# Opening of a diffusion block kernel: constants, modulation and first norm put into one stage

## The chip, the cores and the metric

The kernel runs on one core of a Trainium2 chip. The metric is the device time of one execution in microseconds (us), lower is better; between versions, medians are compared.

## What is computed

Two layers of a block of a diffusion transformer, for 512 latent and 256 context tokens of width 1024, all in float32. Only the opening of a layer matters here: a conditioning vector gives shift, scale and gate vectors through a large matrix (adaLN), and the tokens are RMS-normed, scaled and shifted before the input projection.

```python
def _rms_norm(x, g):
    xf = x.astype(jnp.float32)
    y = xf * lax.rsqrt(jnp.mean(xf * xf, axis=-1, keepdims=True) + EPS)
    return (y * g.astype(jnp.float32)).astype(x.dtype)
```

In each layer: six vectors = silu(c) @ ada_w + ada_b, for the latent tokens from c and for the context tokens from c_ctx; h = rms_norm(x, pre_mix_g) * (1 + scale) + shift; then h @ w_in feeds four attention groups (full, latent, windowed, neighbourhood), whose joined output goes through w_out; a routed mixture of 64 experts (top 8) and one shared expert follows. Shift is the first 1024 columns of ada_w's product and scale the second 1024.

## The kernel before, in words

Each stage is one block: a program for each engine, and a barrier over the engines at its end (in the trace the wait for it appears as `<-PEq L370`, the line where the block before was opened). Inside a stage the engines meet through semaphores; `Signal.wait` waits for a count, `stage_over` moves its base. Everything that SP loads goes through one hardware queue in the order written.

`build` opens with three stages for layer 0:

- `load_all` (L314): SP asks for the conditioning vectors (craw), cst (identity, rotary tables and more, 682 KB), csth and small0 and small1, and waits for the last four. ScalarE computes silu of craw into csil, VectorE fills constants.
- `modulation_start` (L359): shift and scale, 2048 columns of ada_w, come as eight chunks of 256 columns (1 MB each), in order, into four buffers; the load of chunk b waits for the products of chunk b-4. Per chunk, TensorE computes the products (`chunk_products`, L348: eight matmuls with 32 stationary columns, sixteen instructions), ScalarE copies them to SBUF (L400), TensorE turns them into columns (`chunk_columns`, L355), one chunk behind. After the last chunk VectorE adds the bias (L406). SP issues the six token tiles of x (512 KB each, L379) after the chunks.
- `norm_in` (L422): SP loads the first input weights w_in (2 MB). VectorE forms scale and shift (L467 to L469). For each of six tiles of 128 tokens: ScalarE squares and sums a row (L455), VectorE takes the mean (L474), GpSimd the power -0.5 (L500), VectorE scales the row (L479), TensorE transposes eight 128x128 blocks into two PSUM banks (L509, double buffered over tiles), ScalarE copies four of them with scale and shift (L447) and VectorE the other four (L492).

For layer 1 `norm_in` does the same, with shift and scale made earlier. Then `mixer` starts: its first products are L678, tile by tile, released by w_in and the barrier. The opening's buffers in SBUF are freed at the stages' ends.

Of the kernel before, what the change touches and what calls it, by code (L numbers as in the profile page):

```python
# [27 lines left out]
P = 128  # L28
# [63 lines left out]
def build(nc, t, stop=None):  # L92

    ctx = ExitStack()
    with ctx:
# [32 lines left out]
        load_all(env)  # L128
        modulation_start(env)
        for l in range(DEPTH):  # L130
# [183 lines left out]
def load_all(v):  # L314

    nc, S = v.nc, v.S
    loaded, craw_loaded, silu = S("start_loaded"), S("conditioning_loaded"), S("silu_done")
    with ExitStack() as scope:
        craw = v.sb("craw", [P, KD, 2], scope=scope)
        with nc.Block() as block:  # L320
            @block.sync
            def _(sp):
                sp.dma_start(craw[:, :, :], v.t["cvec"]).then_inc(craw_loaded.sem, 16)
                sp.dma_start(v.cst[:, :], v.t["consts"]).then_inc(loaded.sem, 16)
                sp.dma_start(v.csth[:, :], v.t["consts16"]).then_inc(loaded.sem, 16)
                for l in range(DEPTH):
                    sp.dma_start(v.small[l][:, :], v.t["small"][l]).then_inc(loaded.sem, 16)
                sp.wait_ge(loaded.sem, 64)

            @block.vector  # L330
            def _(dve):
                dve.memset(v.half[:, :], -0.5)
                dve.memset(v.csil[:, :, 2:32], 0.0)

            @block.scalar
            def _(act):
                act.wait_ge(craw_loaded.sem, 16)
                act.activation(v.csil[:, :, 0:2], craw[:, :, :], ACT.Silu).then_inc(silu.sem, 1)
    silu.stage_over(1)


# [17 lines left out]
def modulation_start(v):  # L359


    nc, S = v.nc, v.S
    nb = START_CHUNKS
    s_w = [S(f"ada_loaded{i}") for i in range(4)]
    s_mm, s_part, s_col, s_raw = S("ada_summed"), S("ada_partial"), S("ada_turned"), S("mod_columns")
    with ExitStack() as scope:
        aw = [v.sb(f"ada_start{i}", [P, KD, MC], scope=scope) for i in range(4)]
        part = [v.sb(f"ada_part{i}", [P, MC], scope=scope) for i in range(2)]
        pm = v.ps[:, 2, 0:4 * nb]
        with nc.Block() as block:  # L370
            @block.sync
            def _(sp):
                for b in range(nb):

                    s_mm.wait(sp, b - 3)
                    sp.dma_start(aw[b % 4][:, :, :].rearrange("p k n -> p (k n)"), v.t["ada_w"][0, b]).then_inc(s_w[b % 4].sem, 16)
                for i in range(NT):
                    src = v.t["x"][i * P:(i + 1) * P, :] if i < LT else v.t["ctx"][(i - LT) * P:(i - LT + 1) * P, :]
                    sp.dma_start(v.xs[:, i, :], src).then_inc(S(f"ffn_loaded{i}").sem, 16)  # L379

            @block.tensor
            def _(pe):
                def columns(b):
                    s_part.wait(pe, b + 1)
                    chunk_columns(v, pe, part[b % 2], pm[:, 4 * b:4 * b + 4]).then_inc(s_col.sem, 1)

                for b in range(nb):
                    s_w[b % 4].wait(pe, 16 * (b // 4 + 1))
                    s_part.wait(pe, b - 1)
                    chunk_products(v, pe, aw[b % 4], v.ps[:, b % 2, 0:MC]).then_inc(s_mm.sem, 1)  # L390
                    if b:
                        columns(b - 1)
                columns(nb - 1)

            @block.scalar
            def _(act):
                for b in range(nb):
                    s_mm.wait(act, b + 1)
                    s_col.wait(act, b - 1)
                    act.copy(part[b % 2][:, :], v.ps[:, b % 2, 0:MC]).then_inc(s_part.sem, 1)  # L400

            @block.vector
            def _(dve):
                s_col.wait(dve, nb)
                bias = v.small[0][:, S_ADAB:S_ADAB + 2 * nb].unsqueeze(2).broadcast_to([P, 2 * nb, 2])
                dve.tensor_tensor(v.mraw[0][:, 0:2 * nb, :], pm.rearrange("p (j c) -> p j c", c=2), bias, ALU.add).then_inc(s_raw.sem, 1)  # L406
    for s in s_w:
        s.stage_over(16 * (nb // 4))
    for s, k in ((s_mm, nb), (s_part, nb), (s_col, nb), (s_raw, 1)):
        s.stage_over(k)  # L410


# [8 lines left out]

def norm_in(v, l, held, wg):  # L422
# [5 lines left out]
    s_xl = [S(f"ffn_loaded{i}") for i in range(NT if l == 0 else 0)]  # L428
# [84 lines left out]
    for s in s_xl:  # L513
        s.stage_over(16)
# [1514 lines left out]
```

## Time and profile before

| | us |
|---|---|
| median of 3 runs | 2821.33 (2820.92 to 2824.53) |
| the profiled execution | 2827.55 |
| its span in the trace | 2825.7 |
| busy: TensorE / weight loads | 2557.3 (90%) / 1340.5 (47%) |
| busy: VectorE / ScalarE / GpSimd | 1083.8 (38%) / 585.7 (21%) / 387.4 (14%) |
| mean granted TensorE clock | 0.961 |

The span runs from the first to the last instruction; the execution's time has 1.9 us around it. The busy shares are means over stages with different limits: the opening is 51 of 2826 us, and what it is bound by is to be read from its own windows and timelines.

A windows row shows a stretch, its length, the busy time of PE (TensorE's matmuls), PEld (its weight loads), DVE (VectorE), ACT (ScalarE) and POOL (GpSimd) with instruction counts, the TensorE clock that the throttle granted (1.00 is 2.4 GHz, 0.50 is 1.2 GHz), the busy share of the 16 DMA engines and GB/s. A timeline row shows start, duration, engine, source line, instruction, output<-inputs, shape, count merged into the row, and in brackets the idle time before it with what ended it. SPq is SP's queue: its duration is that of issuing.

### The profile page before, as it was taken

To read this page: it belongs to the slowest core of one execution; us is meant where nothing else is said; L and a number is where in the kernel's file an instruction comes from. 1 tells how busy PE (TensorE), PEld (TensorE's weight loads), DVE (VectorE), ACT (ScalarE), POOL (GpSimd) and SP (SyncE) were. 2 spreads that over 40 slices of the span, in tenths; PEclk is the share of its full clock that TensorE was granted. 3 is DMA by queue.
4 is the path that set the end of the run, shared out by engine and by line. 5 is a ranking of instruction groups with operands and counts; after the bars stand their busy time and mean duration, and the time that the engine had idled before them with its cause. 6 is when DMAs were issued, how large, how long until landed. Compare 5 with 4: busy or idle time off the path is not lost. (4 is left out here: it accounts for less than half of the span.)

```text
span 2825.7 us, 42866 instructions
## 1 busy us (share of the span) xinstructions
PE 2557.3 (90%) x12617; PEld 1340.5 (47%) x12618; DVE 1083.8 (38%) x3199; ACT 585.7 (21%) x1378; POOL 387.4 (14%) x314
## 2 busy tenths in 40 slices
PE   6999989999999999999995688989998999899995
PEld 3566555645544444444442366666553433334332
DVE  3443451534333333333333643451452333233323
ACT  3323341411111111111111341331310111111111
POOL 1000001000022222222122200001001121121212
PEclk8999999999999999999998889999998999999997
DMA  7120303043689998999994311212446999998983
GB/s 288 47 94 31 120 16 147 1 183 119 256 272 333 340 337 285 329 339 335 336 349 138 121 40 55 96 45 83 147 173 255 380 400 394 394 391 294 385 307 112
DMA packets 104978, 619.25 MB, mean 219 GB/s; under 512 B 22832, under 2 KB 23088, under 8 KB 64688
## 3 DMA queue, kind: packets, MB, share of 16 engines
q1 hardware_dynamic: 69744, 525.06, 46.9%
q0 software_dynamic: 33696, 87.63, 12.7%
q10 hardware_dynamic: 1440, 5.24, 0.5%
q8 instruction: 63, 1.03, 0.1%
q14 instruction: 35, 0.29, 0.0%
HBM read 578.84 MB, written 77.99 MB: 232 GB/s over the span
## 5 line engine op out<-in xcount | busy, mean ns | idle before, releaser
L1581 PE MATMUL ps<-wgu,xT 128*64 128x512 f32 (+1 forms) x1456 | 454.8, 596 | 0.0
L1581 PE MATMUL ps<-wgu,SGx 128*64 128x512 f32 (+1 forms) x1344 | 348.3, 606 | 18.7 <-DMA wgu<-in_exp_gu 15.6
L1504 POOL DMA_INDIRECT ffn_rows<-Y,six x114 | 182.6, 1602 | 1095.1 <-issue 576.3
L1581 PEld LDWEIGHTS ps<-wgu,xT 128*64 128x64 f32 (+1 forms) x1456 | 173.1, 158 | 229.2 <-issue 224.3
L678 PE MATMUL ps<-w_in,wgu 128*128 128x512 f32 (+3 forms) x768 | 263.9, 503 | 14.8 <-PEq L628 3.8
L1589 PE MATMUL ps<-wd,hiddenT 128*64 128x512 f32 (+1 forms) x736 | 237.9, 599 | 3.5 <-issue 3.4
L1581 PEld LDWEIGHTS ps<-wgu,SGx 128*64 128x64 f32 (+1 forms) x1344 | 118.7, 147 | 208.8 <-issue 201.3
L678 PEld LDWEIGHTS ps<-w_in,wgu 128*128 128x128 f32 x768 | 148.8, 196 | 121.9 <-issue 108.8
L1589 PE MATMUL ps<-wd,csil 128*64 128x512 f32 (+1 forms) x688 | 180.8, 601 | 12.1 <-issue 11.6
L1790 DVE TENSOR_TENSOR hidden<-silu,ps 128x256 f32<-128x256 f32 x64 | 27.0, 421 | 364.5 <-ACT silu L1722 364.5
L1717 ACT ACTIVATE Y<-ps,wc 128x512 f32<-128x512 f32 x114 | 78.4, 687 | 417.4 <-PE ps L1589 417.4
L1784 DVE TENSOR_SCALAR Y<-ps,wc 128x512 f32<-128x512 f32 x114 | 85.6, 751 | 198.6 <-PE ps L1589 198.6
L1555 PEld LDWEIGHTS ps<-cst,X 128*128 128x128 f32 x912 | 101.3, 141 | 108.9 <-DMA X<-h_rows,gix 58.5
L1555 PE MATMUL ps<-cst,X 128*128 128x128 f32 x912 | 123.4, 279 | 26.2 <-DMA X<-h_rows,gix 26.0
L1098 PE MATMUL ps<-w_in,oT 128*128 128x512 f32 x320 | 143.1, 608 | 0.0
L1589 PEld LDWEIGHTS ps<-wd,hiddenT 128*64 128x64 f32 (+1 forms) x736 | 84.4, 159 | 111.1 <-issue 110.8
L1790 DVE TENSOR_TENSOR small<-small,ps 128x256 f32<-128x256 f32 x48 | 20.2, 421 | 299.3 <-ACT small L1722 287.9
L1494 POOL DMA_INDIRECT X<-h_rows,gix x118 | 121.9, 1033 | 86.1 <-issue 35.0
L1722 ACT ACTIVATE silu<-ps 128x256 f32<-128x256 f32 x64 | 24.6, 385 | 417.2 <-PE ps L1581 417.2
L1750 DVE TENSOR_TENSOR mark<-csth,cur 128x384 f16<-128x384 f16 (+1 forms) x236 | 107.7, 497 | 4.0
L1589 PEld LDWEIGHTS ps<-wd,csil 128*64 128x64 f32 (+1 forms) x688 | 61.0, 145 | 99.0 <-issue 98.9
L678 PE MATMUL ps<-w_in,wd 128*128 128x256 f32 (+5 forms) x384 | 102.8, 425 | 0.0
(496 smaller groups left out, 3076.2 us busy)
## 6 DMA issues: line engine op xcount, KB each, us to landing
wgu<-in_exp_gu SPq DMA_DIRECT2D x128, 2048.0 KB
wd<-in_exp_d SPq DMA_DIRECT2D x128, 1024.0 KB, 8.9
wgu<-in_ada_w SPq DMA_DIRECT2D x40, 1024.0 KB, 4.9
ada_start<-in_ada_w SPq DMA_DIRECT2D x8, 1024.0 KB, 8.3
w_in<-in_w_in SPq DMA_DIRECT2D x4, 2048.0 KB, 10.3
w_in<-in_w_out SPq DMA_DIRECT2D x4, 2048.0 KB, 12.5
wgu<-ffn_rows SPq DMA_DIRECT2D x16, 512.0 KB, 8.4
w_in<-in_w_in SPq DMA_DIRECT2D x2, 3072.0 KB, 15.0
```

The lines of the kernel that those rows point to most:

```text
L678: last = pe.matmul(pp[i % 2][:, at:at + c1 - c0], held.columns(k, i), wg[g % 2][:, k, c0:c1], start=(k == 0), stop=(k == KD - 1))
L1098: last = pe.matmul(ps[:, 2 * (i % 2) + n, :], oT[:, k, i * P:(i + 1) * P], w[n][:, k, 0:512], start=(k == 0), stop=(k == KD - 1))
L1494: pool.indirect_dma_start(out=X[j][:, :], out_offset=None, in_=v.h2_dram, in_offset=bass.IndirectOffsetOnAxis(ap=gix[j][:, 0:1], axis=0), ...
L1504: pool.indirect_dma_start(out=v.acc_dram, out_offset=bass.IndirectOffsetOnAxis(ap=six[j][:, 0:1], axis=0), in_=Y[j][:, :], in_offset=None, ...
L1555: last = pe.transpose(ps[:, 3 + k // 4, k % 4 * P:(k % 4 + 1) * P], X[j][:, k * P:(k + 1) * P], v.ident)
L1581: last = pe.matmul(ps[rows_of, 0, :], xT[:, k, rows_of], wgu[b][:, k, :], start=(k == 0), stop=(k == KD - 1))
L1589: last = pe.matmul(ps[rows_of, 1 + c, :], G[:, f, rows_of], wd[b][:, f, c * 512:(c + 1) * 512], start=(f == 0), stop=(f == 1))
L1717: act.activation(Y[j][:, 0:512], ps[:, 1, :], ACT.Copy, scale=wc[j][:, 0:1]).then_inc(y_act, 1)
L1722: act.activation(SG[:, :], ps[:, 0, 0:FD], ACT.Silu).then_inc(silu, 1)
L1750: last = dve.tensor_tensor(mark[:, :, h * HB:(h + 1) * HB], iota, cur[:, :, h:h + 1].broadcast_to([P, nt, HB]), ALU.is_equal)
L1784: dve.tensor_scalar(Y[j][:, 512:D], ps[:, 2, :], wc[j][:, 0:1], None, ALU.mult).then_inc(y_dve, 1)
L1790: dve.tensor_tensor(HID[:, :], SG[:, :], ps[:, 0, FD:2 * FD], ALU.mult).then_inc(hidden, 1)
```

## The change

The stages `load_all`, `modulation_start` and, for layer 0, `norm_in` become one stage, `opening`. `norm_in` stays for layer 1.

- SP's order: craw, cst, small0, the six token tiles, the eight chunks, w_in, csth, small1. The stage starts its work on cst and small0 only; SP waits for csth and small1 at the end.
- Chunks come as pairs: 0 and 4, 1 and 5, 2 and 6, 3 and 7 (shift's columns and scale's columns of the same 256). After a pair, VectorE computes shift and scale for its two 128-column blocks (five dependent steps).
- All six tiles are normed first, into one buffer xn of 6 x 1024. Then, for each pair, TensorE transposes the pair's two column blocks of all tiles (12 transposes) into three PSUM banks, and the copies take whole block rows: one of 128x512 and two of 128x256 by ScalarE, one of 128x512 by VectorE. `turn(j)`, the transposes of pair j, waits for the copies of pair j-1.

```diff
         env = type("Env", (), env)
-        load_all(env)
-        modulation_start(env)
         for l in range(DEPTH):
...
-                norm_in(env, l, held, wg)
+                if l == 0:
+                    opening(env, held, wg)
+                else:
+                    norm_in(env, l, held, wg)
...
+def opening(v, held, wg):
+    nc, S, mods = v.nc, v.S, v.mods
+    nb = START_CHUNKS
+    order = [n * (nb // 2) + j for j in range(nb // 2) for n in range(2)]
...
+        aw = [v.sb(f"ada_start{i}", [P, KD, MC], scope=scope) for i in range(4)]
+        part = [v.sb(f"ada_part{i}", [P, MC], scope=scope) for i in range(2)]
+        xn = v.sb("xn0", [P, NT, D], scope=scope)
+        ss = v.sb("ss0", [P, 3, NT], scope=scope)
+        sums = [v.ps[:, i, 0:MC] for i in range(2)]
+        def columns_of(j, n):
+            return v.ps[:, 2 + j % 2, 4 * n:4 * n + 4]
+        def latent(h):
+            return v.ps[:, 4 + h, :]
+        def context(h):
+            return v.ps[:, 6, h * CT * P:(h + 1) * CT * P]
...
+                sp.dma_start(v.small[0][:, :], v.t["small"][0]).then_inc(loaded.sem, 16)
+                for i in range(NT):
+                    src = v.t["x"][i * P:(i + 1) * P, :] if i < LT else v.t["ctx"][(i - LT) * P:(i - LT + 1) * P, :]
+                    sp.dma_start(v.xs[:, i, :], src).then_inc(s_xl[i].sem, 16)
+                for t, b in enumerate(order):
+                    s_mm.wait(sp, t - 3)
+                    sp.dma_start(aw[t % 4][:, :, :].rearrange("p k n -> p (k n)"), v.t["ada_w"][0, b]).then_inc(s_w[t % 4].sem, 16)
+                load_w_in(v, sp, 0, 0, wg)
+                sp.dma_start(v.csth[:, :], v.t["consts16"]).then_inc(craw_loaded.sem, 16)
+                sp.dma_start(v.small[1][:, :], v.t["small"][1]).then_inc(craw_loaded.sem, 16)
+                craw_loaded.wait(sp, 48)
+            @block.scalar
+            def _(act):
+                def evac(j):
+                    s_t.wait(act, j + 1)
+                    s_mod.wait(act, j + 1)
+                    act.activation(held.rows[0][:, 2 * j, 0:LT * P], latent(0), ACT.Identity,
+                                   scale=mods[:, 0, 0, 2 * j:2 * j + 1], bias=mods[:, 1, 0, 2 * j:2 * j + 1])
+                    for h in range(2):
+                        k = 2 * j + h
+                        last = act.activation(held.rows[1][:, k, 0:CT * P], context(h), ACT.Identity,
+                                              scale=mods[:, 0, 1, k:k + 1], bias=mods[:, 1, 1, k:k + 1])
+                    last.then_inc(s_ea.sem, 1)
...
+                for i in range(NT):
+                    s_xl[i].wait(act, 16)
+                    act.activation(xn[:, i, :], v.xs[:, i, :], ACT.Square, accum_out=ss[:, 0, i:i + 1]).then_inc(s_sq.sem, 1)
+                for t in range(nb):
+                    s_mm.wait(act, t + 1)
+                    s_col.wait(act, t - 1)
+                    act.copy(part[t % 2][:, :], sums[t % 2]).then_inc(s_part.sem, 1)
+                    if t and t % 2 == 0:
+                        evac(t // 2 - 1)
+                evac(nb // 2 - 1)
...
+                for i in range(NT):
+                    s_sq.wait(dve, i + 1)
+                    dve.tensor_scalar(ss[:, 1, i:i + 1], ss[:, 0, i:i + 1], 1.0 / D, EPS, ALU.mult, ALU.add).then_inc(s_ms.sem, 1)
+                    s_rstd.wait(dve, i + 1)
+                    dve.tensor_scalar(xn[:, i, :], v.xs[:, i, :], ss[:, 2, i:i + 1], None, ALU.mult).then_inc(s_xn.sem, 1)
+                loaded.wait(dve, 32)
+                raw = v.mraw[0]
+                for j in range(nb // 2):
+                    of_pair = slice(2 * j, 2 * j + 2)
+                    s_col.wait(dve, 2 * j + 2)
+                    for n in range(2):
+                        b = n * (nb // 2) + j
+                        bias = v.small[0][:, S_ADAB + 2 * b:S_ADAB + 2 * b + 2].unsqueeze(2).broadcast_to([P, 2, 2])
+                        step(dve.tensor_tensor(raw[:, 2 * b:2 * b + 2, :], columns_of(j, n).rearrange("p (k c) -> p k c", c=2), bias, ALU.add))
+                    step(dve.tensor_copy(mods[:, 1, :, of_pair], vector_columns(v, 0, 0)[:, :, of_pair]))
+                    step(dve.tensor_scalar(mods[:, 0, :, of_pair], vector_columns(v, 0, 1)[:, :, of_pair], 1.0, None, ALU.add))
+                    dve.tensor_tensor(mods[:, 0, :, of_pair], mods[:, 0, :, of_pair], gain_columns(v, 0, S_PRE)[:, :, of_pair], ALU.mult).then_inc(s_mod.sem, 1)
+                    s_mod.wait(dve, j + 1)
+                    s_t.wait(dve, j + 1)
+                    k = 2 * j + 1
+                    dve.tensor_scalar(held.rows[0][:, k, 0:LT * P], latent(1), mods[:, 0, 0, k:k + 1], mods[:, 1, 0, k:k + 1],
+                                      ALU.mult, ALU.add).then_inc(s_ed.sem, 1)
...
+                def turn(j):
+                    s_ea.wait(pe, j)
+                    s_ed.wait(pe, j)
+                    for i in range(NT):
+                        if j == 0:
+                            s_xn.wait(pe, i + 1)
+                        for h in range(2):
+                            out = latent(h)[:, i * P:(i + 1) * P] if i < LT else context(h)[:, (i - LT) * P:(i - LT + 1) * P]
+                            last = pe.transpose(out, xn[:, i, (2 * j + h) * P:(2 * j + h + 1) * P], v.ident)
+                    last.then_inc(s_t.sem, 1)
...
+                loaded.wait(pe, 32)
+                silu.wait(pe, 3)
+                turn(0)
+                for t in range(nb):
+                    if t > 2 and t % 2:
+                        turn(t // 2)
+                    s_w[t % 4].wait(pe, 16 * (t // 4 + 1))
+                    s_part.wait(pe, t - 1)
+                    chunk_products(v, pe, aw[t % 4], sums[t % 2]).then_inc(s_mm.sem, 1)
+                    if t:
+                        columns(t - 1)
```

GpSimd takes the power for each tile as before. `columns(t)` turns chunk t's products into columns as before.

## Rows read from the trace of the kernel before

**Rows 1.** Windows by stage: length, each engine's busy us (instructions), PEclk, DMA share, GB/s.

```profile
0.00:7.40 7.40, 0.00 (x0) 0.01 (x1) 0.34 (x3) 1.50 (x2) 0.19 (x4) 1.00 0.58 190
7.40:35.00 27.60, 20.80 (x160) 11.09 (x160) 0.19 (x1) 2.98 (x8) 0.00 (x0) 0.73 0.96 395
...
38.30:51.20 12.90, 8.70 (x48) 7.38 (x48) 11.45 (x34) 12.20 (x32) 4.42 (x5) 0.78 0.33 128
```

**Rows 2.** Timeline, TensorE, 12 to 35 us: start, duration, engine, line, instruction, [idle before].

```profile
12.38 1.94 PE L348 MATMUL ps<-ada_start,csil 128*32 128x256 f32 x16 [12.38 <-DMA ada_start<-in_ada_w]
14.87 1.93 PE L348 MATMUL ps<-ada_start,csil 128*32 128x256 f32 x16 [0.55 <-DMA ada_start<-in_ada_w]
16.73 0.61 PE L355 MATMUL ps<-cst,ada_part 128*128 128x2 f32 x4
17.35 1.07 PE L348 MATMUL ps<-ada_start,csil 128*32 128x256 f32 x16
18.35 0.61 PE L355 MATMUL ps<-cst,ada_part 128*128 128x2 f32 x4
...
25.29 1.93 PE L348 MATMUL ps<-ada_start,csil 128*32 128x256 f32 x16
...
28.09 1.93 PE L348 MATMUL ps<-ada_start,csil 128*32 128x256 f32 x16
```

**Rows 3.** Timeline, TensorE in the norm and the mixer's start; ScalarE's last copies.

```profile
38.39 3.67 PE L509 MATMUL ps<-cst,xn 128*128 128x128 f32 x16 [3.76 <-DVE xn L479]
42.54 1.77 PE L509 MATMUL ps<-cst,xn 128*128 128x128 f32 x8 [0.47 <-DVE xn L479]
44.54 1.10 PE L509 MATMUL ps<-cst,xn 128*128 128x128 f32 x8 [0.23 <-DVE xn L479]
...
51.42 13.97 PE L678 MATMUL ps<-w_in,wgu 128*128 128x512 f32 x32 [1.85 <-PEq L435]
...
47.98 3.14 ACT L447 ACTIVATE wd<-ps,mods 128x128 f32<-128x128 f32 x8
```

**Rows 4.** Windows of the modulation's second half and the norm's first, columns as in rows 1.

```profile
20.20:35.00 14.80, 14.43 (x104) 8.17 (x96) 0.19 (x1) 1.86 (x5) 0.00 (x0) 0.50 1.01 415
35.00:43.90 8.90, 5.03 (x23) 4.64 (x24) 5.83 (x20) 8.10 (x18) 3.54 (x4) 0.50 0.84 309
```

**Rows 5.** Timeline, TensorE, layer 1, 1550 to 1600 us: norm and mixer's start.

```profile
1569.45 3.68 PE L509 MATMUL ps<-cst,xn 128*128 128x128 f32 x16 [42.64 <-DVE xn L479]
...
1582.99 15.86 PE L678 MATMUL ps<-w_in,wgu 128*128 128x512 f32 x32 [1.85 <-PEq L435]
```

**Rows 6.** Timeline, VectorE's steps on the scales, one round of the row chain.

```profile
35.39 0.17 DVE L468 TENSOR_SCALAR mods<-mod_raw 128x16 f32<-128x16 f32 x1
35.60 0.17 DVE L469 TENSOR_TENSOR mods<-mods,small 128x16 f32<-128x16 f32 x1
...
41.68 0.14 DVE L474 TENSOR_SCALAR ss<-ss 128x1 f32<-128x1 f32 x1
41.74 0.74 DVE L479 TENSOR_SCALAR xn<-xs,ss 128x1024 f32<-128x1024 f32 x1
...
41.90 0.99 POOL L500 TENSOR_TENSOR ss<-ss,half 128x1 f32<-128x1 f32 x1 [1.96 <-DVE ss L474]
```

**Rows 7.** Groups by line and form: xcount, busy us, mean ns, idle before.

```profile
L447 ACT ACTIVATE wgu<-ps,mods 128x128 f32<-128x128 f32 x16 | 6.0, 489 | 0.5 <-PE ps L509 0.5
...
L1717 ACT ACTIVATE Y<-ps,wc 128x512 f32<-128x512 f32 x114 | 78.4, 687 | 417.4 <-PE ps L1589 417.4
...
L831 ACT ACTIVATE R_0A<-ps,st_0A 128x256 f32<-128x256 f32 x8 | 3.8, 476 | 3.7 <-DVE st_0A L963 3.7
...
L1784 DVE TENSOR_SCALAR Y<-ps,wc 128x512 f32<-128x512 f32 x114 | 85.6, 751 | 198.6 <-PE ps L1589 198.6
```

**Rows 8.** SP's timeline, first chunk issues; DMA issues by line, KB, median us to landing.

```profile
7.47 14.50 SPq L376 DMA_DIRECT2D ada_start<-in_ada_w  x8
...
cst<-in_consts SPq DMA_DIRECT2D x1, 681.5 KB, 4.0
```

More of the change, by code:

```diff
@@ L311, in load_expert @@
     eng.dma_start(ex.wd[e][:, :, :].rearrange("p k n -> p (k n)"), v.t["exp_d"][l, e]).then_inc(v.S(f"down_landed{e}_{l}").sem, 16)
[L314 to L339, printed above, removed]
 def chunk_products(v, pe, aw, out):
@@ L356, in chunk_columns @@
     return last
[L359 to L410, printed above, removed]
 def gain_columns(v, l, c):
@@ L419, in vector_columns, with _, columns @@
     return v.mraw[l][:, n * KD:(n + 1) * KD, :].rearrange("p k c -> p c k")
+def opening(v, held, wg):
+    nc, S, mods = v.nc, v.S, v.mods
+    nb = START_CHUNKS
+    order = [n * (nb // 2) + j for j in range(nb // 2) for n in range(2)]
+    craw_loaded, loaded, silu = S("conditioning_loaded"), S("start_loaded"), S("silu_done")
+    s_w = [S(f"ada_loaded{i}") for i in range(4)]
+    s_xl = [S(f"ffn_loaded{i}") for i in range(NT)]
+    s_mm, s_part, s_col = S("ada_summed"), S("ada_partial"), S("ada_turned")
+    s_sq, s_ms, s_rstd, s_xn, s_t, s_ea, s_ed = (S("squares"), S("mean_square"), S("rstd"), S("x_normed"), S("turned"),
+                                                 S("turned_by_act"), S("turned_by_dve"))
+    s_mod, s_step = S("scale_shift_ready"), S("dve_step")
+    counts = []
+    with ExitStack() as scope:
+        craw = v.sb("craw", [P, KD, 2], scope=scope)
+        aw = [v.sb(f"ada_start{i}", [P, KD, MC], scope=scope) for i in range(4)]
[9 more added lines that the diff above has]
+            return v.ps[:, 6, h * CT * P:(h + 1) * CT * P]
+        with nc.Block() as block:
+            @block.sync
+            def _(sp):
+                sp.dma_start(craw[:, :, :], v.t["cvec"]).then_inc(craw_loaded.sem, 16)
+                sp.dma_start(v.cst[:, :], v.t["consts"]).then_inc(loaded.sem, 16)
+                sp.dma_start(v.small[0][:, :], v.t["small"][0]).then_inc(loaded.sem, 16)
[21 more added lines that the diff above has]
+                    last.then_inc(s_ea.sem, 1)
+                craw_loaded.wait(act, 16)
+                act.activation(v.csil[:, :, 0:2], craw[:, :, :], ACT.Silu).then_inc(silu.sem, 1)
+                for i in range(NT):
[8 more added lines that the diff above has]
+                evac(nb // 2 - 1)
+            @block.vector
+            def _(dve):
+                step = stepper(dve, s_step, counts)
+                dve.memset(v.half[:, :], -0.5).then_inc(silu.sem, 1)
+                dve.memset(v.csil[:, :, 2:32], 0.0).then_inc(silu.sem, 1)
+                for i in range(NT):
[20 more added lines that the diff above has]
+                                      ALU.mult, ALU.add).then_inc(s_ed.sem, 1)
+            @block.gpsimd
+            def _(pool):
+                silu.wait(pool, 3)
+                for i in range(NT):
+                    s_ms.wait(pool, i + 1)
+                    pool.tensor_tensor(ss[:, 2, i:i + 1], ss[:, 1, i:i + 1], v.half[:, 0:1], ALU.pow).then_inc(s_rstd.sem, 1)
+            @block.tensor
+            def _(pe):
+                def turn(j):
+                    s_ea.wait(pe, j)
+                    s_ed.wait(pe, j)
+                    for i in range(NT):
+                        if j == 0:
[4 more added lines that the diff above has]
+                    last.then_inc(s_t.sem, 1)
+                def columns(t):
+                    s_part.wait(pe, t + 1)
+                    chunk_columns(v, pe, part[t % 2], columns_of(t // 2, t % 2)).then_inc(s_col.sem, 1)
+                loaded.wait(pe, 32)
[9 more added lines that the diff above has]
+                        columns(t - 1)
+                columns(nb - 1)
+    for s, k in ((craw_loaded, 48), (loaded, 32), (silu, 3), (s_mm, nb), (s_part, nb), (s_col, nb), (s_sq, NT), (s_ms, NT), (s_rstd, NT), (s_xn, NT),
+                 (s_t, nb // 2), (s_ea, nb // 2), (s_ed, nb // 2), (s_mod, nb // 2), (s_step, counts[0])):
+        s.stage_over(k)
+    for s in s_w:
+        s.stage_over(16 * (nb // 4))
+    for s in s_xl:
+        s.stage_over(16)
```

5 lines of the change are left out of this document (removed).

## The prediction

> **What bounds the kernel now.** The windows by stage come first: they show what the three stages in question cost and which resource is full in each. The constants take 7.4 us, in which TensorE does nothing and the DMA engines are 0.58 busy; the opening modulation then keeps the DMA at 0.96, 395 GB/s; the norm from 38.3 us on has VectorE at 11.45 and ScalarE at 12.20 of 12.9 us and the DMA at 0.33 [rows 1]. So the idea has room: three stages of different limits in a row, 51.1 us until the last copy of the norm ends and 51.4 us until the mixer's first product [rows 3].
>
> The second view is TensorE's timeline of the modulation. The first two chunks' products are released by their weights, 2.49 us apart, which is the price of a chunk on the DMA side. From 22 us on TensorE is the slower: a chunk starts every 2.80 us (25.29, 28.09), products 1.93 us and its columns the rest. Where the columns at 16.73 took 0.61 and the products at 17.35 took 1.07, the same work cost 1.00 + 0.62 = 1.62 us [rows 2]. The granted clock tells these two prices apart: 0.50 (1.2 GHz) from 20.2 to 35 us, although TensorE was busy 14.43 of 14.80 us, and still 0.50 until 43.9 us [rows 4]. The opening is thus a stage in which the clock is an unknown of the first rank.
>
> The third view is the timeline of the norm. Eight transposes cost 1.77 us at the half clock and 1.10 us at the full one [rows 3], so 0.22 and 0.14 us each.
>
> **The change, part by part.** Removed: the wait for all constants and two stage boundaries. Before, no chunk could be asked for before 7.47 us. The stage now waits for cst and small0 only; csth and small1 go behind the chunks and the first w_in on SP's queue. In exchange six x tiles (3.1 MB) now stand ahead of the chunks.
>
> Step 1, rows normed. Before the first tile SP issues craw, cst and small0 (0.97 MB) and the tile is 0.52 MB: 1.5 MB against the 1.4 MB of constants that had landed when SP went on at 7.47 us, where cst alone took 4.0 us to land [rows 8]. I take 7.3 us for the first tile. Its square costs 1.15 us, so 8.6 us for the first mean square. From there VectorE's own order decides: mean square, wait for GpSimd's power, scale the row, and only then the next tile's mean square. One round is 0.22 us to GpSimd's start, 0.99 us there and 0.74 us for the row (41.68, 41.90, 41.74), 1.95 us [rows 6]. Tiles land every 1.25 us (half a chunk's 2.49), so the chain and not the load sets the pitch: 8.6 + 6 x 1.95 = 20.3 us. The transposes of each tile follow behind its row; only the last two are left, 0.5 us with the hand-over (42.48 to 42.54 is 0.06 us [rows 3, 6]). TensorE begins chunk 0 at **20.8 us**. Its weights are there: 0.97 + 3.15 + 1.05 MB at 421 GB/s from about 2.7 us on is 15 us.
>
> Step 2, TensorE's work. Eight chunks, 8 x 2.81 = 22.5 us at half clock, 8 x 1.62 = 13.0 at full. Three blocks of 12 transposes after the first, 3 x 12 x 0.22 = 8.0 us or 5.0 us.
>
> Step 3, the added wait. Banks 4, 5 and 6 hold one pair of column blocks. turn(j) waits for both copies of pair j-1; those wait for that pair's shift and scale, and these for the columns of its second chunk, which TensorE issues just before. Behind turn(j) in TensorE's order stand the products of chunk 2j+1, so nothing covers the wait. Per pair: hand-over 0.05, five VectorE steps on a pitch of 0.21 us (35.39 to 35.60) 1.05, hand-over 0.05, ScalarE's copies, hand-over 0.05. The copies are one 128x512 (0.69, nearest L1717) and two 128x256 (0.48 each, nearest L831), 1.65 as plain sum; sixteen L447 copies of mean 0.489 fill only 6.0 us, an overlap of 0.115 each, so 1.42 us [rows 6, 7]. VectorE's one copy (0.75, L1784) lies beside them. Bounds 1.3 and 1.65; I take 1.45, so 2.65 us per pair, four times (the last before the stage's end): 10.6 us. The number of copies falls from 24 to 12 on ScalarE, but before they ran beside transposes; now all of them stand on the path.
>
> Sum at half clock: 20.8 + 22.5 + 8.0 + 10.6 = **61.9 us**; at full clock 20.6 + 13.0 + 5.0 + 10.6 = **49.2 us**; before 51.1.
>
> Step 4, the clock between these ends. It rose three times after dense work: between 12.38 and 16.73 (two chunks' products, 4.3 us), between 38.39 and 43.9 (5.5 us), and in layer 1, where sixteen transposes began at 1569.45 at half clock and ran 3.68 us and the next eight took 1.09 [rows 2 to 5]. [...] The dense stretch of a round here is turn(j) plus one chunk's products, 2.66 + 1.93 = 4.6 us. So I expect a rise near its end; columns, products, columns then cost 2.2 instead of 3.7 us, saving 1.5, in the last pair 0.8. The wait of 2.65 us with nothing on TensorE follows, and after the gaps around 17 to 20 us the clock was back at half by 20.2 [rows 2, 4]. All four rounds: -5.3 us; none: 0. I take three of four, with a little for a late rise or an early one: -4.2, an end at **57.7 us**, +6.6.
>
> The Trainium skill, page "TensorE: Matmul & The Clock Gate", Part 4 (PE-mode transpose), says the full clock does not engage for transposes. The trace disagrees: between 35 and 44 us only transposes ran, and they reached 1.10 us for eight [rows 3]. By the rule the sum would be the one at half clock.
>
> Step 5, the mixer behind. Before, its first 32 products found the full clock and took 13.97 us; in layer 1 they found the half clock after a pause and took 15.86 [rows 3, 5]. The stage now ends with columns and a 2.65 us wait: +1.9 (bounds 0 and 2.5).
>
> Step 6, what costs nothing. Chunk loads 4 to 7 wait for products of chunks 0 to 3, the last at about 35 us, and land some 5 us later (7.47 to 12.38 [rows 2, 8]); chunk 7 is wanted past 50 us. w_in, csth and small1 follow it, 3.6 MB in all with the chunk, about 46 us, and SP's final wait with them. Should TensorE be quicker than at the full clock all through, these would be next. Silu, squares and copies of ScalarE (the copy of chunk 0 stands behind the squares, done by 16 us) are covered.
>
> Total: +6.6 + 1.9 = **+8.5 us**. Nothing later is paced by a clock of its own: weights are asked for as buffers come free, so the delay goes through. The profiled execution took 2827.55 us, 6.2 above the median of 2821.33; the difference is added to the median: **2829.8 us**. A measurement of this kernel tells 0.2%, 5.6 us, from no change.
>
> **The rivals.**
> - *The clock never rises in the rounds*: 61.9 us, +10.8 + 1.9 = +12.7, 2834.0. For it: 14.8 us at half with TensorE busy [rows 4]. Against: those were columns and products in turn, a third of it columns; here denser stretches occur. It is also what the page's rule on transposes gives. 0.15.
> - *The clock is full through most rounds*: 49.2 us, -1.9, 2819.4, with a cold start or two near 2822. For it: from 44.5 on short bursts with gaps of over 1 us kept it full [rows 3]. Against: the 2.65 us waits. 0.12.
> - *Faster: the weights set the end, not the rounds.* Place: turn(j). If the copies of pair j-1 did not hold it, a round would be two chunks' loads, 5.0 us. The last chunk would land at 2.7 + 12.5 MB / 421 GB/s = 32.4 us, plus 6.5 us for its products, columns and copies: 39 us, -12, 2809. It decides once a round is under 5.0 us; by the rows it is 7.6 at full and 10.9 at half clock. 0.05.
> - *x does not come first*: if the queue's transfers shared the engines, six tiles and four chunks (8.3 MB) would land together at 22.5 us and the chain of step 1 would begin 15 us late: +24, 2845. Against: cst landed after 4.0 us and chunk 0 at 12.38 with three behind it [rows 2, 8]. 0.03.
>
> **How the numbers follow.** The forecast has 0.65; its own range is +4.5 (all rises, mixer less cold, copies at 1.3) to +12: 2825.8 to 2833.3. 0.13 of it I put within 5.6 us. Slower by over 0.2%: 0.52 + 0.15 + 0.03 = 0.70; within: 0.13 + 0.12 = 0.25; faster 0.05. The range takes in the half-clock case with its unknown copies and stops short of the full-clock one: 2823 to 2835.5; left out are 0.05 + 0.03 + 0.12.
>
> **What would show it.** Chunk 0's products start near 21 us with their weights long landed; the scaled rows stand 1.95 us apart; three gaps of about 2.7 us on TensorE, each ended by ScalarE's copies; the granted clock near 0.5 to 0.65 from 21 to 58 us; the mixer's first product at 58, its first 32 lasting over 15 us. The mixer starting before 50 us, or turn(j) released by weights or by the rows, would make the prediction wrong.

## The result and the profile after

Timed in turn on the same chips, the changed kernel took 2830.65 us (median of 22 runs, 2828.54 to 2837.71) and the kernel before 2825.93 us (22 runs, 2820.92 to 2833.65). The ratio is 1.002, with a 95% interval of 1.0013 to 1.0026: slower by 5.7 us (3.7 to 7.3). The change is a small loss, right at the bound that a measurement tells from none. The forecast was 2829.8 us and +8.5; part of the agreement in the absolute time is that the three runs shown of the kernel before lay 4.6 us below its later median, so it is the difference that has to be judged. The profiled execution took 2829.81 us (span 2828.0).

The waits of TensorE from 18 us, where the chunks begin, to the mixer:

```profile
PE ps L462 <- ACT wd L400: 8.6, 3, 2.9
PE ps L741 <- PEq L374: 3.1, 1, 3.1
PE ps L462 <- DVE xn L426: 0.8, 1, 0.8
```

Three waits of 2.8 to 2.9 us for ScalarE's last copy, and one of 3.1 us for the stage's end, of which 2.8 us pass until ScalarE's last copy ends at 57.70. No wait is for weights; the 0.8 us for a row ends at 18.00, ahead of chunk 0. TensorE's timeline of the same stretch (start, duration, engine, line, instruction, idle before):

```profile
18.62 3.64 PE L321 MATMUL ps<-ada_start,csil 128*32 128x256 f32 x32
...
23.14 1.93 PE L321 MATMUL ps<-ada_start,csil 128*32 128x256 f32 x16
...
25.00 1.01 PE L328 MATMUL ps<-cst,ada_part 128*128 128x2 f32 x4
...
28.93 2.82 PE L462 MATMUL ps<-cst,xn 128*128 128x128 f32 x12 [2.91 <-ACT wd L400]
...
33.55 0.61 PE L328 MATMUL ps<-cst,ada_part 128*128 128x2 f32 x4
...
34.09 1.07 PE L321 MATMUL ps<-ada_start,csil 128*32 128x256 f32 x16
...
38.53 2.82 PE L462 MATMUL ps<-cst,xn 128*128 128x128 f32 x12 [2.84 <-ACT wd L400]
...
41.28 1.94 PE L321 MATMUL ps<-ada_start,csil 128*32 128x256 f32 x16
...
43.15 0.91 PE L328 MATMUL ps<-cst,ada_part 128*128 128x2 f32 x4
...
58.01 15.39 PE L741 MATMUL ps<-w_in,wgu 128*128 128x512 f32 x32 [3.09 <-PEq L374]
```

Chunk 0 starts at 18.62 us, 2.2 us earlier than in the sum. Both prices of [rows 2] stand side by side: products at 1.94 and at 1.07 us, columns at 1.01 and at 0.61. The clock rose inside the second and the third round, behind a block of 12 transposes and one chunk's products (33.55, and within the columns at 43.15), and not in the first and the last. The mixer starts at 58.01 us against 51.42 [rows 3], and its first 32 products take 15.39 us instead of 13.97.

Where the clock rose and fell is read here from these prices. The granted clock of the windows (columns as in [rows 1]) agrees with them from 36.9 us on, and not before:

```profile
18.60:33.50 14.90, 11.99 (x85) 6.85 (x84) 1.64 (x6) 2.81 (x6) 0.00 (x0) 1.00 0.80 331
33.50:36.90 3.40, 2.19 (x28) 1.46 (x24) 0.99 (x6) 0.86 (x3) 0.00 (x0) 1.00 0.64 198
36.90:43.60 6.70, 5.07 (x31) 3.47 (x31) 0.64 (x1) 1.89 (x4) 0.00 (x0) 0.51 1.02 392
43.60:47.20 3.60, 1.99 (x23) 1.31 (x23) 1.39 (x6) 0.94 (x3) 0.00 (x0) 0.97 0.23 76
47.20:58.00 10.80, 6.49 (x36) 4.82 (x37) 1.87 (x7) 3.24 (x7) 0.00 (x0) 0.50 0.00 0
```

Up to the first fall that it shows, the granted clock reads 1.00, while chunks cost 1.93 us until 33.5 us, the same price as later at 0.50. The kernel before has this too: its first two chunks took 1.94 and 1.93 us [rows 2] at a granted clock of 1.00 (window 12.38 to 15.00; 0.99 in 15.00 to 20.20). So the prediction's sentence that the granted clock tells the two prices apart holds from 20.2 us on only, and ahead of the first fall in a trace only the price of an instruction can be read. Twice the clock fell inside a wait of TensorE: at 37.0 us, 1.3 us after its last instruction, and at 47.2 us, 1.6 us after it.

The path through one wait, VectorE and ScalarE in the timeline:

```profile
26.13 0.36 DVE L435 TENSOR_TENSOR mod_raw<-ps,small 128x4 f32<-128x4 f32 x2 [8.18 <-PE ps L328]
...
26.93 0.17 DVE L438 TENSOR_TENSOR mods<-mods,small 128x4 f32<-128x4 f32 x1
...
27.19 0.78 ACT L396 ACTIVATE wgu<-ps,mods 128x512 f32<-128x512 f32 x1 [1.68 <-DVE mods L438]
27.87 1.01 ACT L400 ACTIVATE wd<-ps,mods 128x256 f32<-128x256 f32 x2
```

From the last columns of the pair (26.0 us) to the next transposes (28.93) nothing runs on TensorE: 1.0 us of VectorE's five steps, 1.7 us of ScalarE's three copies. And the row chain, one tile:

```profile
12.17 0.55 POOL L450 TENSOR_TENSOR ss<-ss,half 128x1 f32<-128x1 f32 x1 [0.93 <-DVE ss L424]
...
12.76 0.75 DVE L426 TENSOR_SCALAR xn<-xs,ss 128x1024 f32<-128x1024 f32 x1 [0.66 <-POOL ss L450]
```

GpSimd's power takes 0.55 us here, not the 0.99 of [rows 6], and a round, from one row's power to the next one's, is 1.48 us. The kernel before has this price too, at its first tile, where VectorE is idle:

```profile
36.66 0.55 POOL L500 TENSOR_TENSOR ss<-ss,half 128x1 f32<-128x1 f32 x1 [36.23 <-DVE ss L474]
```

### The profile page after: what moved, and what is told of

Read it like the earlier page. It is cut to its first block and busy times, and to the rows that moved or that the text cites. A ratio compares the mean times of both kernels' runs of the same rounds, so it can differ in the third digit from the quotient of the medians.

```text
span 2828.0 us, 42822 instructions
## 1 busy us (share of the span) xinstructions
PE 2556.6 (90%) x12617; PEld 1337.7 (47%) x12618; DVE 1081.2 (38%) x3195; ACT 584.0 (21%) x1366; POOL 385.0 (14%) x314
## 5 line engine op out<-in xcount | busy, mean ns | idle before, releaser
L1853 DVE TENSOR_TENSOR small<-small,ps 128x256 f32<-128x256 f32 x48 | 20.2, 421 | 300.4 <-ACT small L1785 300.4
```

The lines of the kernel that those rows point to most:

```text
L1853: dve.tensor_tensor(HID[:, :], SG[:, :], ps[:, 0, FD:2 * FD], ALU.mult).then_inc(hidden, 1)
```

## The experiments

In all kernels built for this section three expressions in TensorE's program for the experts are written `& (VAR - 1)` instead of `% VAR`; VAR is 256, so the value is the same. The first table gives what the sections below refer to. "Rest" is the span less the mixer's start; the ratio is against the kernel before in the same call.

| run | mixer's first product, us | its first 32, us | span | rest | median, us (runs) | ratio (95%) |
|---|---|---|---|---|---|---|
| before | 51.4 | 13.97 | 2825.7 | 2774.3 | 2825.93 (22) | |
| c0_before, control | 52.2 | 13.97 | 2819.8 | 2767.6 | 2826.38 (12) | 0.9999 (0.9988 to 1.001) |
| changed | 58.0 | 15.39 | 2828.0 | 2770.0 | 2830.65 (22) | 1.002 (1.0013 to 1.0026) |
| c1_after, again | 57.5 | 16.86 | 2828.1 | 2770.6 | 2829.88 (10) | 1.0015 (1.0006 to 1.0024) |
| e1_two_sets | 43.6 | 15.64 | 2814.0 | 2770.4 | 2817.38 (9) | 0.9969 (0.9957 to 0.9981) |
| e2_filler | 48.1 | 13.97 | 2817.6 | 2769.5 | 2820.27 (12) | 0.9979 (0.9969 to 0.9989) |
| e3_sets_rows | 43.2 | 15.67 | 2814.0 | 2770.8 | 2815.85 (7) | 0.9965 (0.9951 to 0.9978) |
| e4_delay | 78.5 | 13.97 | 2853.4 | 2774.9 | 2854.72 (6) | 1.0096 (1.0081 to 1.011) |
| e5_all | 42.1 | 13.97 | 2818.1 | 2776.0 | 2819.61 (12) | 0.9977 (0.9968 to 0.9986) |
| e6_constants | 49.6 | 15.67 | 2820.7 | 2771.1 | 2820.39 (12) | 0.9977 (0.9967 to 0.9987) |
| e8_no_end_wait | 43.6 | 13.97 | 2808.6 | 2765.0 | 2818.06 (10) | 0.9974 (0.9961 to 0.9986) |
| e9_constants_again | 48.9 | 15.67 | 2820.8 | 2771.9 | 2821.84 (12) | 0.9981 (0.9971 to 0.9992) |

### The two controls

Expected of the kernel before:

> The kernel before once more, with the same two words of the TensorE wait masked as in all these runs. It shows what the mask costs and how far one kernel's stages differ from one profile to the next. Expected by every theory: ratio 1.000 give or take 0.001; mixer's first product at 51.4 to 52.6 us (the delayed kernel's transposes ended 1.1 us later than in the profile of before); the stages behind the opening equal to within 3 us.

Expected of the changed kernel:

> The changed kernel once more; only the two words of a TensorE wait in the expert loop are masked with & (VAR - 1) instead of % VAR, the same value by the same number of instructions. Theory A (the opening delays the mixer by 6 to 7 us, and a part of it is lost again in layer 1): mixer's first product at 58 us give or take 1.5, the phase of the clock's rises differing from run to run; ratio to the kernel before near 1.002. Rival B (the delay passes through whole): ratio near 1.003.

Measured: 0.9999 (0.9988 to 1.001) and 1.0015; the mask costs nothing that can be told. In the control one stretch of the modulation differs from [rows 2]:

```profile
16.73 1.02 PE L355 MATMUL ps<-cst,ada_part 128*128 128x2 f32 x4
17.67 1.93 PE L348 MATMUL ps<-ada_start,csil 128*32 128x256 f32 x16
...
52.22 13.97 PE L678 MATMUL ps<-w_in,wgu 128*128 128x512 f32 x32 [1.85 <-PEq L435]
```

The third chunk's products take 1.93 us where they took 1.07, and the mixer starts 0.8 us later. The repeat of the changed kernel shows the same freedom; here the clock rose in the first round, and the mixer's start is 57.55 us:

```profile
22.70 0.61 PE L328 MATMUL ps<-cst,ada_part 128*128 128x2 f32 x4
...
57.55 16.86 PE L741 MATMUL ps<-w_in,wgu 128*128 128x512 f32 x32 [3.09 <-PEq L374]
```

So the opening costs 57.8 - 51.8 = 6.0 us by the means of two profiles each. What a single profile says of the whole span is worth less: the two profiles of the kernel before differ by 5.9 us, with 6.7 us in the rest, where the expectation was 3 us at most. Of c1's two theories, 1.0015 speaks for A; the interval (up to 1.0024) leaves B's 1.003 out. Whether a part "is lost again" is taken up by e4.

### e1_two_sets: the waits of turn(j) taken away

```diff
-            return v.ps[:, 2 + j % 2, 4 * n:4 * n + 4]
+            return v.ps[:, n, MC + 4 * j:MC + 4 * j + 4]
-        def latent(h):
-            return v.ps[:, 4 + h, :]
+        def latent(j, h):
+            return v.ps[:, 2 + 3 * (j % 2) + h, :]
-            return v.ps[:, 6, h * CT * P:(h + 1) * CT * P]
+            return v.ps[:, 4 + 3 * (j % 2), h * CT * P:(h + 1) * CT * P]
...
+                    s_part.wait(dve, min(2 * j + 3, nb))
...
-                    s_ea.wait(pe, j)
-                    s_ed.wait(pe, j)
+                    s_ea.wait(pe, j - 1)
+                    s_ed.wait(pe, j - 1)
...
+                    if t > 2 and t % 2:
+                        s_step.wait(pe, 4 * (t // 2 - 1) + 2)
```

> The transposed pair has two sets of three PSUM banks, so turn(j) waits for the copies of pair j-2 instead of j-1; the columns move into the free halves of the two sum banks, and the products of chunk 3, 5 and 7 wait for VectorE to have read the pair before. All else as changed. Theory A (the three uncovered waits of about 2.9 us are what makes the opening long): the waits of TensorE before L462 fall from 2.9 us to under 0.3 us, the mixer starts 8.7 us earlier, at 49.3 us at equal clock, and earlier still (46 to 48) if denser work keeps the full clock; ratio 0.999 to 1.000 against the kernel before. Rival B (the copies or the weights bind behind the waits): TensorE waits for chunk weights or for ScalarE's copy of the sums instead, and the mixer starts after 54 us.

Measured: mixer at 43.6 us, 14 us earlier than in the changed kernel, ratio 0.9969. TensorE's waits from 18 us on:

```profile
PE ps L744 <- PEq L374: 3.1, 1, 3.1
PE ps L463 <- DVE xn L426: 0.8, 1, 0.8
PE ps L328 <- ACT ada_part L412: 0.2, 1, 0.2
```

and its timeline:

```profile
25.86 2.80 PE L463 MATMUL ps<-cst,xn 128*128 128x128 f32 x12
28.59 1.68 PE L321 MATMUL ps<-ada_start,csil 128*32 128x256 f32 x16
...
30.74 1.07 PE L321 MATMUL ps<-ada_start,csil 128*32 128x256 f32 x16
...
32.21 1.51 PE L463 MATMUL ps<-cst,xn 128*128 128x128 f32 x12
...
43.59 15.64 PE L744 MATMUL ps<-w_in,wgu 128*128 128x512 f32 x32 [3.09 <-PEq L374]
```

The three waits are gone (one of 0.2 us stands in their place). That is 8.4 us of 14.4. The other 6 us are the clock: by the prices it rose at about 30 us and stayed until the last columns, so that the third and fourth blocks of transposes cost 1.51 us instead of 2.82 and the last four chunks were all at 1.07. (The granted clock reads 1.00 over this whole stretch and first falls at 43.5 us, so it can't confirm the rise; the prices do.) Theory A is confirmed, and its second half more strongly than written (43.6, not 46 to 48; ratio 0.9969, not 0.999 to 1.000): **the waits cost twice, once as idle time and once as half clock behind them**.

### e2_filler: the waits kept, TensorE busy in them

```diff
+                def filler(n, i=0):
+                    for k in range(n):
+                        pe.transpose(v.ps[:, 7, 0:P], xn[:, i, k % KD * P:(k % KD + 1) * P], v.ident)
                 def turn(j):
+                    if j:
+                        filler(14)
...
+                        if j == 0 and i < NT - 1:
+                            filler(3)
...
                 columns(nb - 1)
+                filler(14)
```

> As changed, but TensorE fills its waits: 3 transposes into the unused bank 7 behind each of the first five tiles of turn(0), 14 before turn(1), turn(2), turn(3) and 14 behind the last columns. The results are the same. Theory A (the half clock costs the opening up to 11 us and is due to the pauses; transposes count as activity): granted clock at full from about 19 us to the mixer, chunk pitch 1.62 us, turn 1.65 us, mixer's first product at 47 us (18.4 + 13.0 + 5.0 + 4 x 2.9 = 48), its first 32 products in 14.0 us instead of 15.4; ratio 0.998. Rival B (by the rule of the Trainium skill, page TensorE: Matmul & The Clock Gate, Part 4, transposes do not bring the full clock): the clock stays as it was, the filler at half clock takes 3.1 us and reaches past the waits of 2.9, mixer's first product at 58 to 59 us, ratio 1.002.

Measured: mixer at 48.1 us with its first 32 products in 13.97, ratio 0.9979. L456 is the filler, L468 the kernel's own transposes:

```profile
13.23 0.69 PE L468 MATMUL ps<-cst,xn 128*128 128x128 f32 x2
13.71 0.69 PE L456 MATMUL ps<-cst,xn 128*128 128x128 f32 x3
14.71 0.44 PE L468 MATMUL ps<-cst,xn 128*128 128x128 f32 x2 [0.30 <-DVE xn L426]
...
23.44 1.73 PE L456 MATMUL ps<-cst,xn 128*128 128x128 f32 x14
26.49 1.53 PE L468 MATMUL ps<-cst,xn 128*128 128x128 f32 x12 [1.33 <-ACT wd L400]
...
48.10 13.97 PE L750 MATMUL ps<-w_in,wgu 128*128 128x512 f32 x32 [1.51 <-PEq L374]
```

Up to 14 us TensorE has run nothing but transposes, and the next two take 0.44 us instead of 0.69: the clock rose on transposes alone. It fell once more: the granted clock is 0.50 from 17.6 us, inside the second of two pauses of 0.7 us, to 20.9 us. From 21 us to the mixer every price is the one at full clock and the granted clock is 1.00. The forecast of 47 to 48 us is met by 0.1, and the half clock is thereby priced in the changed kernel: 58.0 - 48.1 = 9.9 us of its opening, of which 0.3 us are an earlier landing of the first x tile (its square starts at 7.39 instead of 7.72 us). The page's rule on transposes (Part 4 of "TensorE: Matmul & The Clock Gate" in the Trainium skill) does not hold for these float32 transposes.

### e3_sets_rows: the row chain as well

```diff
+                mean_square(0)
                 for i in range(NT):
+                    if i + 1 < NT:
+                        mean_square(i + 1)
                     s_rstd.wait(dve, i + 1)
```

> The two bank sets of the run before, and VectorE takes the next tile's mean square ahead of scaling a row, so that GpSimd's power lies beside the scaling. Theory A (the row chain of 1.48 us a tile is on the path to chunk 0, because TensorE begins turn(0)'s last transposes and chunk 0 behind it): rows stand 1.25 us apart, the pace at which x lands, chunk 0 starts at 17.3 instead of 18.6 us, the mixer at 42.4 instead of 43.6 at equal clock; ratio 0.9965. Rival B (something else sets chunk 0's start, such as the landing of x): no earlier than 18.3 us.

Measured: chunk 0 at 17.98 us, mixer at 43.2, ratio 0.9965. Rows stand 1.28 us apart, about as expected, but chunk 0 moved by 0.6 us only, between the two theories:

```profile
10.42 0.99 POOL L456 TENSOR_TENSOR ss<-ss,half 128x1 f32<-128x1 f32 x1 [0.65 <-DVE ss L424]
...
10.26 0.74 DVE L431 TENSOR_SCALAR xn<-xs,ss 128x1024 f32<-128x1024 f32 x1
...
11.54 0.74 DVE L431 TENSOR_SCALAR xn<-xs,ss 128x1024 f32<-128x1024 f32 x1
...
17.98 3.64 PE L321 MATMUL ps<-ada_start,csil 128*32 128x256 f32 x32
```

The power is back at 0.99 us, since it now lies beside VectorE's scaling of a row. The first x tile is squared at the same time as in the changed kernel (7.73 and 7.72 us), but its row is scaled at 10.26 instead of 9.79: by the new order VectorE waits first for the second tile's square. So of the 1.0 us that five shorter rounds give, 0.5 is lost at the first row, and the last row stands at 16.55 instead of 17.20 us. The pitch of 1.28 us is ScalarE's: from the second tile on VectorE's mean squares wait for its squares, which follow one another 1.28 us apart. The gain is small, 0.6 us at chunk 0 and 0.4 at the mixer; between the changed kernel and its repeat chunk 0's start differs by more (18.62 and 19.37 us, with the first square at 7.72 and 8.47).

### e5_all and e8_no_end_wait: how far the terms add

e5 is e3 with the filler of e2 behind the tiles (bank 5) and behind the last columns (bank 2, once the copies of the third pair are done); e8 is e5 with SP's last wait moved out of the stage:

```diff
-                craw_loaded.wait(sp, 48)
...
+                if l == 0 and g == 0:
+                    sp.wait_ge(S("conditioning_loaded").sem, 48)
```

> Both of these and the idle transposes: 3 behind each of the first five tiles (bank 5) and 14 behind the last columns (bank 2). Theory A (waits, row chain and clock are separate terms that add): chunk 0 at 17.3 us, all eight chunks at the full clock, 17.3 + 13.0 + 5.0 + 3.2 = 38.5, mixer's first product at 38.5 to 40 us with its first 32 in 14.0 us; the last weights land at 33 us and are not waited for long; ratio 0.9955. Rival B (at that pace the weights bind): TensorE waits for chunks 5 to 7 or w_in, mixer after 42 us.

> As the run with both bank sets, pipelined rows and idle transposes, but SP waits for csth and small1 in the first mixer instead of at the end of the opening. Theory A (in that run the stage ended 1.5 us behind its last copy because SP waited for the end of its queue): mixer's first product at 40.9 to 41.2 us instead of 42.1, or a wait for w_in of under 1 us; ratio 0.9965. Rival B (w_in lands last anyway and TensorE waits for it): mixer's first product at 41.8 us or later, released by the transfer of w_in.

Measured: mixer at 42.1 and 43.6 us, ratios 0.9977 and 0.9974. In e5 the opening is the shortest of all, but by 1.1 us, not by 4; TensorE's timeline shows what took the place of the waits:

```profile
19.02 1.07 PE L321 MATMUL ps<-ada_start,csil 128*32 128x256 f32 x16 [0.32 <-DMA ada_start<-in_ada_w]
...
21.51 1.07 PE L321 MATMUL ps<-ada_start,csil 128*32 128x256 f32 x16 [0.89 <-DMA ada_start<-in_ada_w]
...
32.52 1.07 PE L321 MATMUL ps<-ada_start,csil 128*32 128x256 f32 x16 [0.43 <-DMA ada_start<-in_ada_w]
...
42.12 13.97 PE L758 MATMUL ps<-w_in,wgu 128*128 128x512 f32 x32 [2.70 <-PEq L374]
```

Chunks at full clock are too quick for the weights: three of them wait, 1.6 us in sum, and behind the second wait the clock fell (granted 0.50 from about 24 to 26.5 us), which made the next block of transposes 2.39 us and the next chunk 1.81. In e8 three chunks wait 2.5 us in sum, one of them 1.40 us, after which the clock is at half until the columns at 34.65 (granted 0.50 from 28 to 34.6 us). In e8's timeline:

```profile
27.52 1.73 PE L321 MATMUL ps<-ada_start,csil 128*32 128x256 f32 x16 [1.40 <-DMA ada_start<-in_ada_w]
...
30.05 2.80 PE L471 MATMUL ps<-cst,xn 128*128 128x128 f32 x12
```

e5's rival B holds: TensorE waits for weights, and the mixer starts after 42 us. Of the last 2.70 us before e5's mixer 1.2 are SP's: its last copy ends at 40.61 us and the mixer starts 1.5 us behind it, where in e8 (43.29) and e1 (43.28) it starts 0.3 us behind. So A of e8 holds for SP's wait, while its mixer came later, at 43.6 us, for the weights' and the clock's sake; that start is B's, but w_in was not what released it. Neither is better at the end than e1 or e3. **e3, 0.9965, that is -9.9 us (6.2 to 13.9), is the lowest ratio of the versions run**, ahead of both kernels; against e1, e5 and e8 the intervals overlap, so which of these is best is not shown.

### e4_delay: does a delay of the opening reach the end?

```diff
+                for k in range(32 if l == 0 else 0):
+                    pe.matmul(v.ps[:, 7, :], v.ident, xn[:, 1, 0:512], start=True, stop=True)
```

> The kernel before, with 32 idle products of 128x512 (about 27.5 us at full clock) on TensorE behind the last transpose of the norm of layer 0; the first ones lie beside the last copies, so the mixer of layer 0 starts about 25.5 us later. Theory A (a delay of the opening passes through to the end whole): +25.5 us, ratio 1.0090. Rival B (some 3 us or more of any delay are taken up later, as the changed kernel's +6.6 at the mixer and +8.3 at layer 1 but +2.2 at the end hint): +22 us or less, ratio 1.0078 or less.

TensorE's timeline, the idle products and the mixer's first:

```profile
50.56 27.63 PE L512 MATMUL ps<-xn,cst 128*128 128x512 f32 x64
78.49 13.97 PE L680 MATMUL ps<-w_in,wgu 128*128 128x512 f32 x32 [0.30 <-PEq L435]
```

Measured: mixer 78.5 - 51.8 = 26.7 us later, median ratio 1.0096, +27.1 us (22.9 to 31.1). B's ratio of 1.0078 or less lies outside the interval (from 1.0081), and the delay passes through as far as can be told; A. The idea that a few us are always taken up later came from the changed kernel's single profile (+6.6 at the mixer, +8.2 at layer 1's norm, +2.3 at the end). The middle value speaks against it, but 3 us less than 26.7 would still lie inside the interval, so a small loss of that kind is not excluded.

### e6_constants and e9_constants_again: one part of the change alone

The kernel before with `load_all` folded into `modulation_start`:

```diff
+                sp.dma_start(craw[:, :, :], v.t["cvec"]).then_inc(craw_loaded.sem, 16)
+                sp.dma_start(v.cst[:, :], v.t["consts"]).then_inc(loaded.sem, 16)
+                sp.dma_start(v.small[0][:, :], v.t["small"][0]).then_inc(loaded.sem, 16)
                 for b in range(nb):
...
+                sp.dma_start(v.csth[:, :], v.t["consts16"]).then_inc(craw_loaded.sem, 16)
+                sp.dma_start(v.small[1][:, :], v.t["small"][1]).then_inc(craw_loaded.sem, 16)
...
+                loaded.wait(pe, 32)
+                silu.wait(pe, 3)
```

> The kernel before with one part of the change alone: constants and modulation in one stage, chunks asked for right behind craw, cst and small0, csth and small1 behind x and waited for at the end of the norm; rows, transposes and copies as before. Theory A (the wait for the constants is worth what TensorE starts earlier by): first products at 7.7 instead of 12.4 us, mixer at 46.7 instead of 51.4 to 52.5 us, -4.7; ratio 0.9983; so the change's other parts cost 11 us. Rival B (the stage behind waits for x, which lands behind the chunks): the squares wait, and the mixer starts after 49 us.

> The kernel with constants and modulation in one stage, unchanged, again: its mixer began only 1.8 us earlier than before and cold, yet its median was 6.6 us lower. Theory A (the opening is worth about 2 us, and the rest was chance in the later stages): ratio 0.9985 to 1.000. Rival B (something behind the opening is systematically shorter): ratio near 0.9977 again, and the profile's later stages shorter than those of the control by 3 us or more.

TensorE's timeline in e6, first chunk and the norm's start:

```profile
9.09 1.94 PE L319 MATMUL ps<-ada_start,csil 128*32 128x256 f32 x16 [9.09 <-DMA ada_start<-in_ada_w]
...
35.89 3.65 PE L496 MATMUL ps<-cst,xn 128*128 128x128 f32 x16 [3.83 <-DVE xn L466]
```

Measured: first products at 9.09 us, not 7.7, mixer at 49.6 and 48.9 us: 2.5 us gained against 51.8, not 4.7. The gain at chunk 0 is 3.3 us; here the sum of e6 was too optimistic, by the landing of chunk 0 (1.4 us). These 3.3 us reach the norm whole where the modulation ran at one price throughout, as in e6 and in the control (first transposes at 35.89 against 39.19 us), and with e9 the mixer (48.9 against 52.2). What makes the mean gain smaller is the clock: the kernel before had one chunk at 1.07 us [rows 2], and e6 its last eight transposes at half clock. The medians, 0.9977 and 0.9981, that is -6.5 us (3.7 to 9.3) and -5.4 us (2.3 to 8.2), are lower than an opening of -2.5 us gives, the more so as both mixers start cold (15.67 us). The profiles' rests (2771.1, 2771.9) lie between the two of the kernel before (2774.3, 2767.6) and name no stage. e9's interval takes in the ratios of both its theories, and its rest is 4 us longer than the control's, not 3 us shorter as B wanted. This difference of some 3 us stays open. What is shown is that this part alone beats the kernel before, and that the rest of the change, at single-buffered banks, turns it into a loss: 57.8 against 49.2 us.

## Why the prediction was right, step by step

The direction and the cause were right: the mixer's start was forecast at 58.0 us (57.7 and the barrier's 0.3) and came at 58.01 and 57.55. That close a hit is luck, made of errors that cancel: chunk 0 2.2 us early, transposes 0.3 us dearer, the four waits 0.8 us longer, and the clock's rises worth 1.2 us less than summed.

- **Step 1, rows normed**: chunk 0 at 18.62 us, not 20.8. The term mis-sized is GpSimd's power: 0.99 us was read from rows where VectorE scales a tile beside it, while here it waits. With 0.55 a round is 1.48 us, six of them 2.8 us less; the first tile came 0.4 us later than summed (7.72 us, not 7.3). The power of the first tile in the kernel before, at 36.66 us, showed the shorter price and was not used.
- **Step 2, TensorE's work**: 2.80 and 1.54 us a chunk, summed as 2.81 and 1.62; 2.75 us for 12 transposes at half clock (38.53 to 41.28 us), 0.1 more each.
- **Step 3, the added wait**: 2.8 to 2.9 us instead of 2.65, four times, +0.8. ScalarE's copies took 1.69 us instead of 1.45, just over the upper bound of 1.65; the overlap read from short copies did not carry over. That the waits are uncovered, that nothing else ends them and what they cost is shown by e1.
- **Step 4, the clock**: rises in two rounds of four (three in the repeat) saved 3.0 us instead of 4.2: from 18.62 us the work at half clock and the waits would be 22.5 + 8.3 + 11.4 = 42.1 us, and it took 39.1 to the last copy at 57.7. The clock was named as the unknown of the first rank, and e2 shows that it is worth up to 10 us. The sign in the prediction, a granted clock near 0.5 to 0.65 from 21 to 58 us, reads 0.76 in the trace, because the first stretch is shown as 1.00; by the prices 7 of the 37 us were at full clock, which makes 0.59 (an estimate).
- **Step 5, the mixer behind**: +1.4 and +2.9 us in the first 32 products, forecast +1.9 with an upper bound of 2.5, which the repeat exceeded.
- **Step 6**: TensorE never waited for weights or w_in in the changed kernel.
- **The total**: +8.5 was forecast, 5.7 (3.7 to 7.3) measured, and 4.2 (1.7 to 6.8) in the repeat. What is too large is the last line of the sum, the opening's delay plus the cold mixer taken whole to the end. The opening's own +6.6 is against one profile of the kernel before; against the mean of its two profiles it is +6.0. That alone lies inside both intervals; with the 1.4 and 2.9 us of the cold mixer it would be 7.4 to 8.9 us, outside both. The cold start of the mixer is real in its stage, but the profiles can't follow it to the end: e1 (cold) and e2 (warm) have rests of 2770.4 and 2769.5, and the rests of equal kernels differ by 6.7 us. The medians of e1 and e2 would fit a cold start that is paid whole (2.9 us apart, where the mixers' starts differ by 4.5 and the cold one lost 1.7), but each ratio is known to about 3 us only. Whether it is given back is open.

Of the rivals, the one with the clock never rising (2834.0) and the one with it full throughout (2819.4) frame what happened. e2 is the second of them, made by hand: its opening ended 1.4 us earlier than the rival's (48.1 us against 49.2 and the barrier's 0.3), and against the kernel before it was 5.9 us faster (3.1 to 8.8), not 1.9. The faster rival, in which the weights set the end once turn(j) is not held, was right in its condition: with that wait gone the opening fell under the kernel before (e1, e3). But in e1 and e3 TensorE waited at no chunk for its weights; only with the filler as well (e5, e8) did the weights bind, and e5's last copy ended at 40.6 us, not at 39.

## What to carry to other kernels

When stages are merged so that one engine turns pieces for others to copy, give the pieces two sets of buffers before anything else; a round in which the producer waits for its own consumers costs that wait each time, and on TensorE it cost again here as half clock in the work behind. In this opening the same merge was a loss with these waits bare, a gain with them filled by idle transposes (e2), and a larger gain, though not clear of e2's, with them gone (e1, e3). A price is to be read from a row in which the neighbouring engines do what they will do in the new order: the power cost 0.99 or 0.55 us by that alone. And a change of 6 us in 2826 is read from its own stage in two profiles of each kernel: the rest of the span differs by that much from one execution to the next.

## What the runs showed of the hardware

GpSimd's power of one element a row took 0.55 us with VectorE idle and 0.99 us, in five of the six tiles of e3, beside VectorE's 0.74 us scaling of a 128x1024 row in SBUF; the power ended 0.41 us after the scaling did (10.26 + 0.74 = 11.00, 10.42 + 0.99 = 11.41). The Trainium skill, page "SBUF — State Buffer", section "Who interferes with whom", says that VectorE operations of this kind can take a pair of ports that they share with GpSimd, and that the later of the two then waits for the other's end; the lengthening agrees with that, and no run here looks at the ports themselves.

The clock rose during transposes alone: by the prices in e2 at about 14 us, and by the granted clock in the kernel before, where it was 0.50 until 43.9 us and 1.00 from 44.0 on, with nothing but transposes on TensorE since 38.39. One pause for weights of 1.40 us in e8 was followed by half clock for the next 7 us. And pauses of about 3 us did not always end in half clock: e5's mixer ran its first 32 products in 13.97 us behind 2.70 us of nothing, e1's in 15.64 us behind 3.09.

In these traces the granted clock reads 1.00 up to its first fall, also where instructions cost what they cost later at 0.50: in e6 the chunks from 9.09 to 24 us took 1.93 us each at 1.00.
